# The last attention head taken out of the loop on two engines, with its last two modulation parts moved into the output tiles

## The chip, the cores and the metric

The kernel runs on one core of one Trainium2 chip. The metric is the device time of one execution in microseconds (us), shown as the median of several runs. The core's engines are TensorE (PE, matmuls; its weight loads are shown as PEld), VectorE (DVE), ScalarE (ACT), GpSimd (POOL) and SyncE (SP, which here only issues transfers). Each works through its own list of instructions and waits for the others at semaphores.

## The reference

Two layers of a diffusion backbone over 256 latent and 256 context tokens of width 2048: a neighbourhood attention with 16 heads, then a Mamba-2 SSD mixer, then an RMS norm. Each layer first derives shift, scale and gate from a conditioning vector:

```
mod = silu(c) @ ada_w + ada_b;  shift, scale, gate = split(mod, 3)
h = rms_norm(x, norm_w) * (1 + scale) + shift
x = x + gate * mixer(h)          # attention: (o * silu(z)) @ w_out
```

All is float32. `ada_w` of a layer is 2048 x 6144. The modulation of the second layer (and the gate of the first) does not depend on x.

## The kernel before, in words

Every large product is made of three matmuls with operands split into a rounded high part and the rest. A weight tile of 2048 x 128 is loaded by SP into a raw slot (1 MB), ACT copies it rounded into `w_hi` (`split_hi`, L353 and L901), DVE subtracts to get `w_lo` (`split_lo`, L357), and PE runs 48 matmuls per tile (`project`, L373, L375, L377), k = 0 to 15 with three each. Tiles 0 to 63 are q, k, v and z of the 16 heads, tiles 64 to 79 the output projection. Two raw slots, two `w_hi` and two `w_lo` are used in turn; tile 66 goes through a pair of its own, `w_third` (L945 on ACT, L1544 on DVE).

Beside these tiles a second piece of work runs that needs no PE. The modulation matrix-vector products are made in units of 512 columns, one unit per head, eight parts per unit. For part l, POOL issues the 512 KB load (`load_ada`, L605), DVE adds the latent half into `ada_acc` (`ada_part(l)`, L1415 and L1421, two instructions), ACT scales the context half into `ada_prod` (`products(l)`, L858, two instructions), and POOL adds those two rows into `acc` (`add_products(l)`, L614 or L620). There is one `ada_prod`, so `products(l)` waits until POOL has added part l - 1 (semaphore `s_gp`); `load_ada(l)` waits until both DVE and ACT have read part l - 2. The counters run through all units, so the order must be kept. After unit h, `ada_sums(h)` (L1432, L1436) reduces both accumulators.

Heads 1 to 15 (counted from 0) are issued one per turn: in turn i of the loop the projections of head i are made while the attention of head i - 1 is finished. Turns 2 to 15 are a hardware loop on each engine (`head` on ACT and DVE, `head_sums` on POOL). Behind the loop comes the seam to the output projection. There ACT copies the gated attention output rounded into `act_hi` (L953, one instruction for each k), DVE subtracts into `act_lo` (`o_low`, L1527), and the attention of head 15 (scores, softmax, exponentials, transposes, values) is done in between. PE runs tile 64 for k = 0 to 14 as `act_lo` comes, turns the probabilities (L2100, L2104), runs tile 65 for k = 0 to 14 with the values of head 15 (L2115) in its middle, and closes both with k = 15. Each output tile t then has an `out_tile` on DVE (`split_lo` of tile t + 1 from the third on, then the residual update L1562) and on ACT (`split_hi` of the next, copy of x L969, square L972). POOL adds the squares (L693) behind a memset of their sum (L688). One unit of modulation, unit 16, is spread over output tiles 0 to 7: `ada_part(t)` and `products(t)` behind tile t.

The order on each engine is written out by hand; there is no scheduler.

Of the kernel before, what the change touches and what calls it, by code (L numbers as in the profile page):

```python
# [27 lines left out]
KT = D // P  # L28
# [6 lines left out]
HEADS = 16  # L35
# [76 lines left out]
def trunk(nc, x, c, ctx, c_ctx, na_norm_w, na_ada_w, na_ada_b, na_w_in, na_rpb, na_w_out,  # L112
# [3 lines left out]
    with es:  # L116
# [275 lines left out]
        def backwards(v):  # L392

            return v.rearrange("p (r w) -> p r w", w=GRID_W)[:, :, ::-1]
# [370 lines left out]
        def _(act):  # L765
            step = Steps(act, act_step)
# [63 lines left out]
            def z_tanh_a(last):  # L830
                act.wait_ge(s_used, last.at(4))
                nc.scalar.activation(z_th, bank[1][:, :], ACT.Tanh, scale=0.5).then_inc(s_th, 1)
# [35 lines left out]
                act.wait_ge(s_vtr, i)  # L868
                nc.scalar.activation(v_hi.rearrange("p a b -> p (a b)"), bank[3][:, :], ACT.Copy).then_inc(s_vhi, 1)

            def head(t1, t4):

                i = t1.i
                z_tanh_a(Turn(i, 4, -4))
                split_hi(act, 1 + 4, Turn(i, 4, -4), 1, i * 32 + (16 - 16 * PRE // 2))
                exp_scores(Turn(i, 3, -3))
                products(0, t1)
                act.wait_ge(s_used, t4.at(1))
                nc.scalar.activation(q_hi, backwards(bank[0][:, :]), ACT.Copy, scale=QSCALE).then_inc(s_qhi, 1)
                next_hi(2, t4)  # L880
                turned_probs(Turn(t1.i, 1, -1))
                v_high(i)
                for l in range(1, 4):
                    products(l, t1)
                act.wait_ge(s_used, t4.at(2))
                nc.scalar.activation(k_hi, bank[1][:, :], ACT.Copy).then_inc(s_khi_k, 1)
                next_hi(3, t4)
                for l in range(4, 6):
                    products(l, t1)
                act.wait_ge(s_used, t4.at(3))  # L890
                nc.scalar.activation(v_t, bank[0][:, :], ACT.Copy).then_inc(s_free[0], 1)
                next_hi(4, t4)
                for l in range(6, 8):
                    products(l, t1)

            def next_hi(j, t4):
# [33 lines left out]
                    products(l, Turn())  # L930

            first_heads()
            with act.Fori(2, HEADS) as i:
                head(Turn(i, 1), Turn(i, 4))
            for k in range(KT):
                if k == 8:
                    z_tanh_a(Turn(base=60))
# [13 lines left out]
                    act.wait_ge(s_used, N_OUT_A)  # L951
                act.wait_ge(s_og, k + 1)
                nc.scalar.activation(act_hi3[:, k, :], o_t[:, k, :], ACT.Copy).then_inc(s_ohi, 1)  # L953


            def gained(u, t2, i):
# [296 lines left out]
        def _(dve):  # L1253
            step = Steps(dve, dve_step)
# [215 lines left out]
                dve.wait_ge(s_khi_k, last1.at(1))  # L1470
                nc.vector.tensor_tensor(k_lo, src[:, :], k_hi.bitcast(F32), ALU.subtract).then_inc(s_free[1], 1)

            def head(t1, t4):
                i = t1.i
                l1, l3 = Turn(i, 1, -1), Turn(i, 3, -3)
                z_gate_a(l1)
# [14 lines left out]
                for l in range(4, 6):  # L1491
                    ada_part(l, t1)
                split_lo(dve, 4, t4, 0)
                for l in range(6, 8):
                    ada_part(l, t1)

            def first_heads():
# [22 lines left out]
                    ada_part(l, none)  # L1520

            first_heads()
            with step.loop(2, HEADS, 14) as i:
                head(Turn(i, 1), Turn(i, 4))
            def o_low(k):
                dve.wait_ge(s_ohi, k + 1)
                nc.vector.tensor_tensor(act_lo3[:, k, :], o_t[:, k, :], act_hi3[:, k, :].bitcast(F32),  # L1527
                                        ALU.subtract).then_inc(s_olo, 1)
# [4 lines left out]
            for k in range(6):  # L1533
                o_low(k)
            softmax(Turn(base=15))
            for k in range(6, KT - 1):
                o_low(k)
# [4 lines left out]
            v_low(Turn(base=15))  # L1542
            dve.wait_ge(s_hi, N_OUT_A + 3)
            nc.vector.tensor_tensor(w_third[1], raw[0], w_third[0].bitcast(F32), ALU.subtract).then_inc(s_lo, 1)  # L1544
            dve.wait_ge(s_gsum, 1)
            for s in range(2):
                ada_columns(0, s, mod_a[:, 2, s, :], colk[:, V_NAB + 32:V_NAB + 48]).then_inc(s_gate, 1)
# [19 lines left out]
            turned = region(30, 512)  # L1567
            last = Turn(HEADS, 1)
            out_tile(0, Turn(), None)
            ada_sums(HEADS - 2, turned)  # L1570
            ada_part(0, last)
            for t in range(1, 8):
# [829 lines left out]
```

## Time and profile before

| | us |
|---|---|
| median of 3 runs | 2068.76 (2068.4 to 2070.06) |
| the profiled execution, its own time | 2066.29 |
| its span in the trace | 2064.4 |
| PE busy | 2011.2 (97% of the span) |
| DVE busy | 1454.2 (70%) |
| ACT busy | 968.8 (47%) |
| POOL busy | 699.0 (34%) |
| PE share of the chain that ended last | 80% |

The span is what the trace covers; 1.89 us of the execution lie around it. In the trace a row stands for one instruction or for several alike, with its start, its duration, and in brackets the idle time ahead of it and who ended that. PE rows overlap: within a tile one matmul of 512 columns starts 0.23 us after the one before. The seam lies at about 863 to 906 us of the span, the first output tiles with modulation parts at 906 to 987 us.

### The profile page before, as it was taken

To read this page: it belongs to the slowest core of one execution; us is meant where nothing else is said; L and a number is where in the kernel's file an instruction comes from. 1 tells how busy PE (TensorE), PEld (TensorE's weight loads), DVE (VectorE), ACT (ScalarE), POOL (GpSimd) and SP (SyncE) were. 2 spreads that over 40 slices of the span, in tenths; PEclk is the share of its full clock that TensorE was granted. 3 is DMA by queue.
4 is the path that set the end of the run, shared out by engine and by line. 5 is a ranking of instruction groups with operands and counts; after the bars stand their busy time and mean duration, and the time that the engine had idled before them with its cause. 6 is when DMAs were issued, how large, how long until landed. Compare 5 with 4: busy or idle time off the path is not lost.

```text
span 2064.4 us, 30995 instructions
## 1 busy us (share of the span) xinstructions
PE 2011.2 (97%) x10458; PEld 1673.0 (81%) x10458; DVE 1454.2 (70%) x2076; ACT 968.8 (47%) x1398; POOL 699.0 (34%) x568
## 2 busy tenths in 40 slices
PE   5999999999999999999999999999999999999998
PEld 3568888888888888878878888888888888888886
DVE  5248787777777777774358878787878787788544
ACT  3244455444544445544365454445444544456443
POOL 1036566555555656526100221212212122120011
PEclk8999999999999999999999999999999999999999
DMA  9996666666666666655353654555555546456654
GB/s 352 342 263 168 179 176 167 172 173 178 177 172 177 173 179 177 148 155 149 107 148 100 161 141 133 140 139 137 132 140 143 148 117 161 127 144 208 226 183 152
DMA packets 422706, 349.23 MB, mean 169 GB/s; under 512 B 13600, under 2 KB 366464, under 8 KB 422016
## 3 DMA queue, kind: packets, MB, share of 16 engines
q1 hardware_dynamic: 397552, 273.43, 45.8%
q0 software_dynamic: 19968, 70.26, 14.2%
q10 hardware_dynamic: 5136, 4.89, 0.7%
q8 instruction: 28, 0.46, 0.1%
q14 instruction: 22, 0.18, 0.0%
HBM read 344.21 MB, written 4.33 MB: 169 GB/s over the span
## 4 chain that ended last, share of the span: by engine, by line
PE 80%; DVE 7%; issue 4%; ACT 3%; DMA 3%; SPq 1%; POOL 1%; DVEq 0%; ACTq 0%; POOLq 0%
PE bank L373 20%; PE bank L377 20%; PE bank L375 20%; DMA arena<-in_na_ada_w_dram 3%; PE bank L2316 3%; PE bank L2318 2%; PE bank L2317 2%; PE bank L2115 1%; DVE w_lo L357 1%; PE bank L2249 1%; ACT w_hi L353 1%; DVE arena L1654 1%; PE bank L2230 1%; PE bank L2030 1%; PE bank L2244 1%
## 5 line engine op out<-in xcount | busy, mean ns | idle before, releaser
L373 PE MATMUL bank<-act_hi,w_hi 128*128 128x512 f32 (+1 forms) x2448 | 903.0, 369 | 9.0 <-DVE w_lo L357 4.7
L377 PE MATMUL bank<-act_hi,w_lo 128*128 128x512 f32 (+1 forms) x2448 | 888.3, 363 | 0.0
L375 PE MATMUL bank<-act_lo,w_hi 128*128 128x512 f32 (+1 forms) x2448 | 888.1, 363 | 0.0
L357 DVE TENSOR_TENSOR w_lo<-arena,w_hi 128x2048 fp32r<-128x2048 f32 x184 | 440.3, 2393 | 272.5 <-ACT w_hi L353 209.1
L373 PEld LDWEIGHTS bank<-act_hi,w_hi 128*128 128x128 f32 x2448 | 462.8, 189 | 80.8 <-DVE w_lo L357 6.4
L377 PEld LDWEIGHTS bank<-act_hi,w_lo 128*128 128x128 f32 x2448 | 462.3, 189 | 73.4
L375 PEld LDWEIGHTS bank<-act_lo,w_hi 128*128 128x128 f32 x2448 | 463.0, 189 | 68.9
L620 POOL TENSOR_TENSOR acc<-acc,arena 128x512 f32<-128x512 f32 x224 | 328.0, 1464 | 123.1 <-ACT arena L858 113.8
L353 ACT ACTIVATE w_hi<-arena 128x2048 fp32r<-128x2048 f32 x138 | 262.9, 1905 | 88.1 <-PE bank L2318 77.9
L858 ACT ACTIVATE arena<-arena,cond_c 128x512 f32<-128x512 f32 x256 | 171.3, 721 | 253.1 <-POOL acc L620 152.5
L1421 DVE SCALAR_TENSOR_TENSOR arena<-arena,cond_c 128x512 f32<-128x512 f32 x240 | 244.1, 1017 | 59.7 <-DMA arena<-in_ssd_ada_w_dram 38.1
L728 POOL TENSOR_TENSOR arena<-arena 128x1024 f32<-128x1024 f32 x32 | 77.1, 2410 | 433.0 <-ACT arena L1060 403.6
L1654 DVE SCALAR_TENSOR_TENSOR arena<-arena,convc 128x512 f32<-128x512 f32 (+1 forms) x192 | 145.7, 759 | 21.3 <-ACT arena L1044 7.1
L1060 ACT ACTIVATE arena<-arena 128x1024 f32<-128x1024 f32 x32 | 33.9, 1060 | 153.2 <-DVE arena L1706 153.2
L2316 PE MATMUL bank<-w_hi,act_hi 128*128 128x512 f32 x256 | 101.1, 395 | 1.9 <-DVE w_lo L357 1.9
L2318 PE MATMUL bank<-w_hi,act_lo 128*128 128x512 f32 x256 | 99.8, 390 | 0.0
L2317 PE MATMUL bank<-w_lo,act_hi 128*128 128x512 f32 x256 | 99.7, 389 | 0.0
L717 POOL TENSOR_SCALAR_AFFINE_SELECT arena<-arena 128x256 f32<-128x256 f32 (+1 forms) x32 | 22.0, 721 | 205.6 <-ACT arena L1178 205.6
L734 POOL TENSOR_TENSOR acc<-acc,arena 128x256 f32<-128x256 f32 x32 | 71.1, 2222 | 43.4 <-ACT arena L1086 43.4
L901 ACT ACTIVATE w_hi<-arena 128x2048 fp32r<-128x2048 f32 x43 | 82.1, 1909 | 0.0
L1049 ACT ACTIVATE arena<-arena 128x512 f32<-128x512 f32 (+1 forms) x48 | 28.6, 596 | 113.7 <-DVE arena L1654 113.7
L605 POOL DMA_DIRECT2D arena<-in_ssd_ada_w_dram x96 | 68.5, 714 | 32.7 <-DVE arena L1421 27.2
(253 smaller groups left out, 2168.6 us busy)
## 6 DMA issues: line engine op xcount, KB each, us to landing
arena<-in_ssd_w_in_dram SPq DMA_DIRECT2D x81, 1024.0 KB, 5.9
arena<-in_na_w_in_dram SPq DMA_DIRECT2D x58, 1024.0 KB, 7.2
arena<-in_ssd_ada_w_dram POOLq DMA_DIRECT2D x96, 512.0 KB, 4.0
arena<-in_na_ada_w_dram SPq DMA_DIRECT2D x64, 512.0 KB, 8.1
arena<-in_ssd_w_out_dram SPq DMA_DIRECT2D x32, 1024.0 KB, 5.0
arena<-in_na_ada_w_dram POOLq DMA_DIRECT2D x32, 512.0 KB, 4.1
arena<-in_na_w_out_dram SPq DMA_DIRECT2D x16, 1024.0 KB, 6.2
arena<-cs_scr SPq DMA_DIRECT2D x64, 256.0 KB, 5.9
```

The lines of the kernel that those rows point to most:

```text
L353: nc.scalar.activation(w_hi[:, n0 % 2, :], raw[slot], ACT.Copy).then_inc(s_hi, 1)
L357: nc.vector.tensor_tensor(w_lo[:, n0 % 2, :], raw[slot], w_hi[:, n0 % 2, :].bitcast(F32), ALU.subtract).then_inc(s_lo, 1)
L373: nc.tensor.matmul(out[:, 0:cols], hi[:, w], act_hi3[:, k, 0:cols], start=(k == 0), stop=False)
L375: nc.tensor.matmul(out[:, 0:cols], hi[:, w], act_lo3[:, k, 0:cols], start=False, stop=False)
L377: mm = nc.tensor.matmul(out[:, 0:cols], lo[:, w], act_hi3[:, k, 0:cols], start=False, stop=(k == KT - 1))
L620: nc.gpsimd.tensor_tensor(acc[:, :], acc[:, :], prod[:, h, :], ALU.add).then_inc(s_gp, 1)
L858: m = nc.scalar.activation(prod[:, h, :], ada_buf[l % 2][:, h, :], ACT.Copy, scale=cond_c[:, k, 1:2])
L1421: m = nc.vector.scalar_tensor_tensor(ada_acc, ada_buf[l % 2][:, h, :], cond_c[:, k, 0:1], ada_acc, ALU.mult, ALU.add)
L1654: m = nc.vector.scalar_tensor_tensor(u, xp[:, 0:segs, k:k + LAT], col(48 + 48 * k), u, ALU.mult, ALU.add)
L2316: nc.tensor.matmul(b[:, :], hi, w_hi[:, n % 2, w], start=(k == 0), stop=False)
L2317: nc.tensor.matmul(b[:, :], hi, w_lo[:, n % 2, w], start=False, stop=False)
L2318: mm = nc.tensor.matmul(b[:, :], lo, w_hi[:, n % 2, w], start=False, stop=(k == IT - 1))
```

## The change

On ACT and DVE the loop ends one turn earlier, and the last turn (head 15) stands behind it as plain code with `parts=6`, so without parts 6 and 7 of its modulation unit. On ACT both parts now follow the copy of `act_hi` for k = 14, ahead of `split_hi` of tile 65. On DVE part 6 follows the `w_lo` of tile 66, and part 7 follows `out_tile(0)`, ahead of `ada_sums(14)`. PE, POOL and SP keep their instructions and their order.

```diff
@@ ACT @@
-            def head(t1, t4):
+            def head(t1, t4, parts=8):
...
-                for l in range(6, 8):
+                for l in range(6, parts):
                     products(l, t1)
...
-            with act.Fori(2, HEADS) as i:
+            with act.Fori(2, HEADS - 1) as i:
                 head(Turn(i, 1), Turn(i, 4))
+            head(Turn(HEADS - 1, 1), Turn(HEADS - 1, 4), 6)
             for k in range(KT):
...
                 nc.scalar.activation(act_hi3[:, k, :], o_t[:, k, :], ACT.Copy).then_inc(s_ohi, 1)
+                if k == KT - 2:
+                    for l in range(6, 8):
+                        products(l, Turn(HEADS - 1, 1))
@@ DVE @@
-                for l in range(6, 8):
+                for l in range(6, parts):
                     ada_part(l, t1)
...
-            with step.loop(2, HEADS, 14) as i:
+            with step.loop(2, HEADS - 1, 14) as i:
                 head(Turn(i, 1), Turn(i, 4))
+            head(Turn(HEADS - 1, 1), Turn(HEADS - 1, 4), 6)
...
             nc.vector.tensor_tensor(w_third[1], raw[0], w_third[0].bitcast(F32), ALU.subtract).then_inc(s_lo, 1)
+            ada_part(6, Turn(HEADS - 1, 1))
             dve.wait_ge(s_gsum, 1)
...
             out_tile(0, Turn(), None)
+            ada_part(7, Turn(HEADS - 1, 1))
             ada_sums(HEADS - 2, turned)
```

ACT in the seam, before, from the last copies of `act_hi` to the turned probabilities (L838 and L844 are the exponentials of head 15, L353 is `split_hi` of tile 65, L945 the `w_hi` of tile 66):

```order
L953 ACTIVATE act_hi<-arena 128x512 x4
L838 ACTIVATE arena,small<-bank,small 128x512 x2
L844 ACTIVATE arena,small<-bank,small 128x256 x2
L953 ACTIVATE act_hi<-arena 128x512 x3
L353 ACTIVATE w_hi<-arena 128x2048
L945 ACTIVATE rounded<-arena 128x2048
L865 ACTIVATE rounded<-bank 128x512 x3
```

The same place on ACT in the changed kernel (L858 are `products(6)` and `products(7)`; other lines have moved by one):

```order
L954 ACTIVATE act_hi<-arena 128x512 x4
L838 ACTIVATE arena,small<-bank,small 128x512 x2
L844 ACTIVATE arena,small<-bank,small 128x256 x2
L954 ACTIVATE act_hi<-arena 128x512 x3
L858 ACTIVATE arena<-arena,cond_c 128x512 x4
L353 ACTIVATE w_hi<-arena 128x2048
L946 ACTIVATE rounded<-arena 128x2048
L865 ACTIVATE rounded<-bank 128x512 x3
```

The four scalings of parts 6 and 7 stand directly ahead of the `split_hi` of tile 65.

DVE from `out_tile(0)` to the `split_lo` of tile 67, before (L1562 is the residual update of a tile, L1432 and L1436 `ada_sums(14)`, L1415 and L1421 modulation parts, L357 `split_lo`):

```order
L1562 SCALAR_TENSOR_TENSOR arena<-bank,mod_a,arena 128x256 x2
L1432 STREAM_TRANSPOSE arena<-arena 128x512
L1436 TENSOR_REDUCE bank<-arena 128x16
L1432 STREAM_TRANSPOSE arena<-acc 128x512
L1436 TENSOR_REDUCE bank<-arena 128x16
L1415 TENSOR_SCALAR arena<-arena,cond_c 128x512
L1421 SCALAR_TENSOR_TENSOR arena<-arena,cond_c 128x512
L1562 SCALAR_TENSOR_TENSOR arena<-bank,mod_a,arena 128x256 x2
L1421 SCALAR_TENSOR_TENSOR arena<-arena,cond_c 128x512 x2
L357 TENSOR_TENSOR w_lo<-arena,w_hi 128x2048
```

The same place on DVE in the changed kernel (L1568 is the residual update, L1425 and L1419 modulation parts, L1436 and L1440 `ada_sums(14)`):

```order
L1568 SCALAR_TENSOR_TENSOR arena<-bank,mod_a,arena 128x256 x2
L1425 SCALAR_TENSOR_TENSOR arena<-arena,cond_c 128x512 x2
L1436 STREAM_TRANSPOSE arena<-arena 128x512
L1440 TENSOR_REDUCE bank<-arena 128x16
L1436 STREAM_TRANSPOSE arena<-acc 128x512
L1440 TENSOR_REDUCE bank<-arena 128x16
L1419 TENSOR_SCALAR arena<-arena,cond_c 128x512
L1425 SCALAR_TENSOR_TENSOR arena<-arena,cond_c 128x512
L1568 SCALAR_TENSOR_TENSOR arena<-bank,mod_a,arena 128x256 x2
L1425 SCALAR_TENSOR_TENSOR arena<-arena,cond_c 128x512 x2
L357 TENSOR_TENSOR w_lo<-arena,w_hi 128x2048
```

Two instructions, part 7, have come in behind the first residual update; the rest keeps its order.

## Rows read from the trace of the kernel before

**Rows 1.** Waits of PE from 862 to 906 us: total, times, longest.
```profile
PE bank L373 <- DVE act_lo L1527: 1.5, 1, 1.5
PE bank L373 <- DVE w_lo L357: 1.3, 1, 1.3
```

**Rows 2.** Timeline of PE in the seam: start, duration, engine, line.
```profile
875.13 0.88 PE L2091 MATMUL bank<-rounded 128*128 128x256 f32 x6
...
881.61 0.50 PE L373 MATMUL bank<-act_hi,w_hi 128*128 128x512 f32 x1 [1.46 <-DVE act_lo L1527]
...
890.75 0.50 PE L373 MATMUL bank<-act_hi,w_hi 128*128 128x512 f32 x1 [1.27 <-DVE w_lo L357]
```

**Rows 3.** Timeline of DVE in the seam.
```profile
878.28 0.75 DVE L1367 TENSOR_TENSOR bank<-bank,arena 128x256 f32<-128x256 f32 x2
...
880.87 5.50 DVE L1527 TENSOR_TENSOR act_lo<-arena,act_hi 128x512 fp32r<-128x512 f32 x9
...
888.41 2.29 DVE L357 TENSOR_TENSOR w_lo<-arena,w_hi 128x2048 fp32r<-128x2048 f32 x1
```

**Rows 4.** Timeline of ACT in the seam.
```profile
866.02 1.34 ACT L858 ACTIVATE arena<-arena,cond_c 128x512 f32<-128x512 f32 x2 [1.00 <-DMA arena<-in_ssd_ada_w_dram]
870.98 1.34 ACT L858 ACTIVATE arena<-arena,cond_c 128x512 f32<-128x512 f32 x2 [3.61 <-POOL acc L620]
872.22 4.26 ACT L953 ACTIVATE act_hi<-arena 128x512 fp32r<-128x512 f32 x8
...
879.80 0.69 ACT L838 ACTIVATE arena<-bank,small 128x512 f32<-128x512 f32 x1 [0.27 <-DVE small L1372]
...
883.60 1.92 ACT L353 ACTIVATE w_hi<-arena 128x2048 fp32r<-128x2048 f32 x1
```

**Rows 5.** POOL: L620 over the whole run (ns), then one timeline row.
```profile
L620 POOL TENSOR_TENSOR acc<-acc,arena x224: 1284/1303/3242, 148.2 to 979.7; 128x512 f32<-128x512 f32 x112
867.53 3.41 POOL L620 TENSOR_TENSOR acc<-acc,arena 128x512 f32<-128x512 f32 x2 [0.90 <-ACT arena L858]
```

**Rows 6.** Timeline of DVE from the first output tile on.
```profile
896.79 0.26 DVE L1445 TENSOR_TENSOR mod_a<-bank,colk 128x16 f32<-128x16 f32 x2 [1.50 <-PE bank L2158]
...
905.04 0.88 DVE L1562 SCALAR_TENSOR_TENSOR arena<-bank,mod_a,arena 128x256 f32<-128x256 f32 x2 [3.83 <-PE bank L377]
...
909.16 1.66 DVE L1421 SCALAR_TENSOR_TENSOR arena<-arena,cond_c 128x512 f32<-128x512 f32 x1
...
911.54 1.52 DVE L1421 SCALAR_TENSOR_TENSOR arena<-arena,cond_c 128x512 f32<-128x512 f32 x2
915.35 2.29 DVE L357 TENSOR_TENSOR w_lo<-arena,w_hi 128x2048 fp32r<-128x2048 f32 x1 [2.29 <-ACT w_hi L353]
...
922.49 3.38 DVE L357 TENSOR_TENSOR w_lo<-arena,w_hi 128x2048 fp32r<-128x2048 f32 x1
```

**Rows 7.** Timeline of ACT, then of PE, at output tile 67.
```profile
912.18 1.32 ACT L858 ACTIVATE arena<-arena,cond_c 128x512 f32<-128x512 f32 x2
913.41 1.90 ACT L353 ACTIVATE w_hi<-arena 128x2048 fp32r<-128x2048 f32 x1
...
917.69 0.50 PE L373 MATMUL bank<-act_hi,w_hi 128*128 128x512 f32 x1
```

**Rows 8.** Loads: a POOL issue, an SP issue, L605's landings at 865-871 and 918-919.5 us.
```profile
911.45 0.71 POOL L605 DMA_DIRECT2D arena<-in_ssd_ada_w_dram  x1 [1.17 <-DVE arena L1421]
...
907.02 0.37 SPq L460 DMA_DIRECT2D arena<-in_na_w_out_dram  x1
...
DMA to landing us min/median/max: 4.0/4.0/4.1
...
DMA to landing us min/median/max: 6.8/6.8/6.8
```

**Rows 9.** Stretches: us, each engine's busy time, PEclk (granted clock), DMA share, GB/s.
```profile
28.00:32.00 4.00, 0.36 (x4) 0.00 (x0) 4.00 (x3) 1.48 (x1) 0.00 (x0) 0.93 1.08 367
...
48.00:52.00 4.00, 3.00 (x7) 2.42 (x8) 3.59 (x7) 4.00 (x8) 2.66 (x3) 0.51 1.06 388
```

More of the change, by code:

```diff
@@ L1471, in key_low, with head @@
                 nc.vector.tensor_tensor(k_lo, src[:, :], k_hi.bitcast(F32), ALU.subtract).then_inc(s_free[1], 1)
-            def head(t1, t4):
+            def head(t1, t4, parts=8):
                 i = t1.i
```

## The prediction

> **What bounds the kernel now.** I read the page's shares first: PE is busy for 97% of the span, so only what makes PE wait can be won or lost. The waits of PE in the seam come next [rows 1]. Two are long enough to matter: 1.5 us for an `act_lo` and 1.3 us for a `w_lo`. The timeline of PE places them [rows 2]: 881.61 is k = 6 of tile 64, 890.75 the first matmul of tile 65. The timelines of DVE and ACT give the reasons [rows 3, 4]. At 881.61 DVE was late: it began the softmax of head 15 (L1367) at 878.28, though the scores were there when L2091 ended at 876.01 (875.13 + 0.88), since it first had six `o_low` to do, and those had begun only behind part 7. At 890.75 DVE was late again: it began the `w_lo` of tile 65 at 888.41, and ACT had its `w_hi` ready at 885.52. So DVE sets the end of the seam, with ACT 2.9 us ahead of it. From 906 us on no PE wait is listed, but one place is tight: tile 67's first matmul starts at 917.69, and its `w_lo` ended at 917.64 (915.35 + 2.29) [rows 6, 7].
>
> **Part by part, the start of the seam.** Taking parts 6 and 7 off the last turn frees ACT and DVE some 5 us earlier. The first eight `act_hi` (L953), at 872.22 before, can run while PE is still in tile 63 and six `o_low` with them. The rest of `act_hi` waits for z as before. DVE is then free when the scores end, and the softmax starts at 876.06, 2.22 us earlier. The first wait of PE goes: `o_low` for k = 6, begun at 880.87, begins at 878.65 and ends at 879.33, and PE wants it at about 880.0 (881.61 less the wait of 1.46, and less a little for which the overlap of matmuls does not show). Gain there 1.5 to 1.7 us, if nothing else follows.
>
> **What is late next.** ACT follows the softmax: exponentials at 877.58 instead of 879.80, and it is done with k = 14 at 881.38, 2.22 us ahead of the 883.60 at which `split_hi` of tile 65 began [rows 4]. There now stand `products(6)` and `products(7)`, and between them ACT must wait for POOL to add part 6, since `ada_prod` is single. The old place shows the price whole: 866.02 to 870.98 from the one to the other, and 1.24 us more until ACT went on at 872.22, 6.20 us together, of which POOL's two adds are 3.41 [rows 4, 5]. So `split_hi` of tile 65 starts at 883.60 - 2.22 + 6.20 = 887.58. From a `split_hi` to the end of the `w_lo` behind it, with DVE waiting, takes 917.64 - 913.41 = 4.23 us [rows 6, 7]. That gives 891.81, and PE starts tile 65 at about 891.86 instead of 890.75: **1.11 us later**, with both old waits turned into one of some 4 us (PE is through with tile 64 and its transposes at 890.75 - 1.27 = 889.48 now, 1.6 earlier then). The bounds come from L620: two adds at its least, 1.284 us each, make the block 5.36 us and the shift +0.27; one at its largest, 3.242, with an ordinary one, makes it +2.3 [rows 5]. I take 3.41, what an add took at the old place, with DVE as busy beside it as it will be at the new one.
>
> Part 6 on DVE behind the `w_lo` of tile 66 costs 1.5 us (two L1421, 1.52) [rows 6]. It fits: DVE stood idle there for 1.50 us before L1445 and for two more before it gates the output, and the last `o_low` was ready 2.8 us before PE reached k = 15. Nothing, unless DVE is 3 us later than I think. POOL's list is unchanged, but its load for part 0 of unit 16 now waits for that part 6, and its add of part 7 comes behind it at about 900 us. ACT wants `ada_prod` again at 907 or later, so this costs nothing.
>
> **The output tiles.** Everything behind tile 64 is 1.11 us later. Then part 7 stands between `out_tile(0)` and `ada_sums(14)`: DVE ends it at 905.92 + 1.11 + 1.45 = 908.48. In the queue behind it are `ada_sums(14)`, part 0, `out_tile(1)`; ACT's square of tile 1, `products(1)` and `split_hi` of tile 67 wait for that one, and PE for the `w_lo`. With 0.05 us of slack, all 1.45 us reach PE: 1.11 + 1.45 = 2.56 us.
>
> A second thing waits for part 7: POOL's `load_ada(1)` of unit 16, since the slot is the one part 7 is read from. Before it was issued at 875 us and had 35 us to land. Now it is issued about 0.6 us behind part 7 (as 911.45 follows the end of part 0 at 910.82, 909.16 + 1.66), at 909.1. SP's 1 MB load of a weight tile, 907.02 before, goes out at 908.1, just ahead of it. How long the part's load takes is in the rows: 4.0 us with the transfers idle, 6.8 us for the one issued at 918.7, 0.8 us behind such a 1 MB load [rows 8]. I take 6.8, the nearer case: it lands at 915.9, where `products(1)` could have started at 912.18 + 2.56 = 914.7. So ACT starts it 3.7 us later than before, and the `w_lo` of tile 67 and PE with it: **+3.7 us** in all, the new PE wait there being 2.7 us. With 4.0 us it is +2.6, with 7.1 +4.0.
>
> The Trainium skill (Trainium Kernel Development and Optimization, Key Constraints) says that transfers from the SP and POOL queues run on the same engines and interleave. By that rule the load shares with the weight tile and the sum is the +3.7; by the idle landing alone it would be +2.6.
>
> Tile 68 recovers: its `w_lo` ended at 925.87, 3.1 us before PE wanted it (917.69 and 48 matmuls 0.23 us apart, 11.3 with the transposes of x), and the two chains move together [rows 6]. Beyond it PE never waits until the next seam, whose work hangs on PE's last output tile. So the shift stays to the end. PE, POOL and SP run the same instructions; the plain copy of the last turn saves and adds only register instructions, which I put at nothing.
>
> **Sum.** +1.1 (tile 65) +1.45 (part 7) +1.15 (landing) = +3.7 us. The profiled execution is 2066.29 us (1.89 around its span) and would be 2070.0; the median of the runs is 2.47 above that execution, so the forecast is 2068.76 + 3.7 = **2072.5 us**. By the bounds of its terms alone, 0.27 + 1.45 = +1.7 to 2.3 + 2.9 = +5.2.
>
> **Rivals.**
> A, the slower clock. PE's new wait, from about 888 to 891.9, comes behind the transposes of the probabilities (1.5 us), so over 5 us pass without a product. In the trace the granted clock fell from 2.4 to 1.2 GHz within the stretch 28 to 32 us (0.93 as its mean), where PE was busy for 0.36 of 4 us, and it was still at half for nearly all of the 3.00 us of PE work at 48 to 52 us [rows 9]. Against it, PE waits less here than there, and the transposes are work too. If the clock falls, 2 to 5 us of work at half rate add 1 to 2.5 us, I take 1.8: +5.5, 2074.3 us. The Trainium skill (TensorE: Matmul & The Clock Gate, Part 4: PE-mode transpose and Why this matters for your kernels) says transposes don't count as busy for the gate and warns of gaps between bursts; by that it would fall here, and the sum would be the +5.5.
> B, the quick landing: the load of part 1 takes about 4 us, the weight tile not being in its way. +2.6, 2071.4 us.
> C, the faster side. ACT had 2.9 us in hand at tile 65. If its block of two parts fitted into them, DVE would carry its 2.22 us through to PE and PE would start tile 65 at 888.5: -2.2; with the load landing early enough and the square of tile 1 not on the path, part 7 would cost nothing, and the time would be 2066.5 us. The start of tile 65 turns from earlier to later at a block of 2.9 + 2.2 = 5.1 us. For it: DVE, and not ACT, sets the end of the seam now. Against it: two scalings of 1.34 and the adds between make 5.36 at the very least.
> D, nothing moves: one of my two chains is read wrongly and gains and losses cancel, 2068.8 us.
>
> **Chances.** Forecast 0.40, A 0.32, B 0.15, C 0.05, D 0.08. A measurement tells about 0.2%, 4.1 us, from no change. The forecast lies just below that (0.3 of it above), A almost wholly above, B and D within. Slower by over 0.2%: 0.12 + 0.30 + 0.03 = 0.45. Faster: C alone stays within, so only with something I have missed, 0.04. Within: 0.51. The range, from B less the spread of the medians (2068.4 to 2070.06) to A at its dearer end: 2070.0 to 2076.3.
>
> **What would show it.** In the profile of the changed kernel: no wait for `act_lo` near 880; softmax of head 15 at 876; four L858 between `act_hi` and `split_hi` of tile 65, with an idle time of about 3.5 us on ACT inside; one PE wait of 3 to 4 us for `w_lo` ahead of tile 65, starting at about 891.9; a PE wait of 1.4 to 3 us ahead of tile 67 at about 921.4, with ACT's `products(1)` released by the load; the clock of the stretch 891 to 895, 1.00 for the forecast, 0.5 for A. Wrong would be a PE that starts tile 65 before 890.7, or a wait at tile 68 or later.

## The result: 0.48% slower, 9.7 us

The changed kernel takes 2079.22 us (median of 6 runs, 2074.76 to 2082.12), the kernel before 2069.55 (6 runs, 2068.4 to 2070.86): ratio 1.0048, 95% interval 1.0038 to 1.0058. The forecast was 2072.5 us, and its range ended at 2076.3. The sign was right, the size was not: less than half of the loss was in the sum. The profiled execution of the kernel before lies 3.3 us below its median, that of the changed kernel 0.3 us above its own.

| | before | after |
|---|---|---|
| median, us | 2069.55 | 2079.22 |
| profiled execution, us | 2066.29 | 2079.52 |
| its span, us | 2064.4 | 2077.9 |
| granted clock, mean | 0.991 | 0.988 |
| PE waits from 862 to 935 us | 2.8 us [rows 1] | 8.6 us |

These are the waits of PE in the changed kernel, in the same view (total, times, longest). Two of PE's three waits are longer than any before, and the third (ahead of the transposes of the probabilities) stands where there was none:

```profile
PE bank L373 <- DVE w_lo L357: 7.3, 2, 4.0
PE bank L2107 <- DVE arena L1389: 1.3, 1, 1.3
```

The timeline of PE says where they are; the rows answer to [rows 2] and to the last of [rows 7]:

```profile
877.87 0.88 PE L2098 MATMUL bank<-rounded 128*128 128x256 f32 x6
...
890.34 1.09 PE L2107 MATMUL bank<-ident,arena 128*128 128x128 f32 x8 [1.32 <-DVE arena L1389]
...
895.08 0.79 PE L373 MATMUL bank<-act_hi,w_hi 128*128 128x512 f32 x1 [3.21 <-DVE w_lo L357]
...
927.65 0.80 PE L373 MATMUL bank<-act_hi,w_hi 128*128 128x512 f32 x1 [4.04 <-DVE w_lo L357]
```

Since PE runs the same list in both kernels, the difference between the starts of one and the same instruction in the two traces is a ledger of the change. Each line is one such instruction; the last column is what the stretch in front of it added.

| PE instruction | before | after | later by | added |
|---|---|---|---|---|
| last scores of head 15 | 875.13 | 877.87 | 2.74 | 2.74 |
| first matmul of tile 65 | 890.75 | 895.08 | 4.33 | 1.59 |
| sums for the modulation | 896.42 | 902.32 | 5.90 | 1.57 |
| first matmul of tile 67 | 917.69 | 927.65 | 9.96 | 4.06 |
| the next sums | 997.49 | 1009.70 | 12.21 | 2.25 |
| head of the SSD stage | 1266.65 | 1277.41 | 10.76 | -1.45 |
| end of its loop | 1715.89 | 1729.54 | 13.65 | 2.89 |

**The first line is not the change's.** 1.4 us of it arose behind a wait of 2.7 us at 141 us, which both kernels have, and after which the clock fell in one of the two executions. The stretch 138 to 144 us of the kernel before, and the same of the changed one (columns as in [rows 9]):

```profile
138.00:144.00 6.00, 3.31 (x15) 2.48 (x14) 5.97 (x6) 5.05 (x6) 3.12 (x4) 1.00 0.99 196
```
```profile
138.00:144.00 6.00, 3.29 (x10) 2.32 (x9) 5.97 (x6) 4.82 (x6) 4.00 (x4) 0.73 0.89 172
```

Of the 13 profiles of this study, all with the same code there, the clock fell at that place in 9 and stayed at 2.4 GHz in 4, and the profile of the kernel before is one of the 4. From there to the seam before_pad (below), which has none of the moves, took 1.4 us longer than the profile of the kernel before, and the changed kernel 1.6. The -1.45 us is no gain of the change either: before_pad has -1.46 over the same stretch. That leaves 12.4 us in this trace for the change, against 9.7 by the medians.

**Tile 65.** ACT's block stands where the forecast put it. Timelines of ACT, POOL and DVE, the rows that answer to [rows 3 to 5]:

```profile
884.12 1.34 ACT L858 ACTIVATE arena<-arena,cond_c 128x512 f32<-128x512 f32 x2
889.56 1.33 ACT L858 ACTIVATE arena<-arena,cond_c 128x512 f32<-128x512 f32 x2 [4.10 <-POOL acc L620]
890.80 1.89 ACT L353 ACTIVATE w_hi<-arena 128x2048 fp32r<-128x2048 f32 x1
```
```profile
885.62 3.85 POOL L620 TENSOR_TENSOR acc<-acc,arena 128x512 f32<-128x512 f32 x2 [16.41 <-ACT arena L858]
```
```profile
887.02 2.74 DVE L1386 TENSOR_SCALAR arena<-arena,small 128x512 f32<-128x512 f32 x2
...
892.73 2.29 DVE L357 TENSOR_TENSOR w_lo<-arena,w_hi 128x2048 fp32r<-128x2048 f32 x1 [1.85 <-ACT w_hi L353]
```

From 884.12 to 890.80 the block takes 6.68 us (forecast 6.20); POOL's two adds are 3.85 (forecast 3.41). These 0.44 us more are nearly all by which tile 65 missed the forecast (1.59 for 1.11). The adds run beside DVE's normalising of the probabilities, which takes 2.74 us for two instructions; over the whole run the same line has (ns, least, middle, most):

```profile
L1386 DVE TENSOR_SCALAR arena<-arena,small x32: 469/486/1502, 161.1 to 888.3; 128x512 f32<-128x512 f32 x32
```

The rows of tile 65's `w_lo` say that DVE then waited 1.85 us for ACT's `w_hi`, so it is ACT's block, and not the normalising, that sets tile 65. The probabilities come late by the normalising, and most of the 2.2 us won at the softmax is gone by PE's transposes, for which PE waits 1.32 us: they start 2.38 us after those of the kernel before, 0.36 less than the 2.74 at the seam's head.

**Tile 67.** ACT, then DVE, the rows that answer to [rows 6, 7], then POOL's load of part 1 of unit 16 with its time to landing, and what stands behind that load in POOL's list:

```profile
915.24 0.63 ACT L976 ACTIVATE arena<-arena 128x512 f32<-128x512 f32 x1 [4.47 <-POOL arena L688]
...
920.05 0.63 ACT L976 ACTIVATE arena<-arena 128x512 f32<-128x512 f32 x1 [2.47 <-DVE arena L1568]
920.73 1.34 ACT L858 ACTIVATE arena<-arena,cond_c 128x512 f32<-128x512 f32 x2
921.97 1.90 ACT L353 ACTIVATE w_hi<-arena 128x2048 fp32r<-128x2048 f32 x1
```
```profile
911.74 1.53 DVE L1425 SCALAR_TENSOR_TENSOR arena<-arena,cond_c 128x512 f32<-128x512 f32 x2
...
916.13 1.41 DVE L1419 TENSOR_SCALAR arena<-arena,cond_c 128x512 f32<-128x512 f32 x1
...
920.73 3.60 DVE L1425 SCALAR_TENSOR_TENSOR arena<-arena,cond_c 128x512 f32<-128x512 f32 x2 [0.71 <-DMA arena<-in_ssd_ada_w_dram]
924.25 3.34 DVE L357 TENSOR_TENSOR w_lo<-arena,w_hi 128x2048 fp32r<-128x2048 f32 x1
```
```profile
913.90 0.71 POOL L605 DMA_DIRECT2D arena<-in_ssd_ada_w_dram  x1 [8.72 <-DVE arena L1425]
914.61 0.54 POOL L688 MEMSET arena<- 128x512 f32 x1
915.96 1.29 POOL L693 TENSOR_TENSOR arena<-arena 128x512 f32<-128x512 f32 x1 [0.81 <-ACT arena L976]
```
```profile
DMA to landing us min/median/max: 6.8/6.8/6.8
```

The load is issued behind part 7 and lands 6.8 us later, at 920.7, as forecast. Counted from the modulation sums, ACT's `split_hi` of tile 67 starts 2.66 us later than before, and the forecast had 2.6 for this place. That it fits is luck, for the load is hardly in it: ACT came to the square of tile 1 only at 920.05 and began `products(1)` 0.68 us behind that, against 0.54 before. What made the rest was on DVE: part 7 took 1.56 us, and the first instruction of part 0 took 1.41 us where it had taken 0.48. It ran beside POOL's addition of tile 0's squares. That addition came so late because POOL's list has the memset (L688) behind `load_ada(1)`, and so behind part 7, and ACT's first square waited 4.47 us for it.

Two more things are new behind that: DVE's part 1 waits 0.71 us for the load and takes 3.60 us where it took 1.52, so the `w_lo` starts 0.4 us behind the end of its `w_hi` (923.87), and it takes 3.34 us in place of 2.29. Together 1.4 us more than the 2.6.

**The clock.** Behind both waits PE works at half rate (1.2 in place of 2.4 GHz) for 3 to 5 us. Stretches of the changed kernel; in the kernel before, PEclk is 1.00 in every stretch from 888 to 936 us:

```profile
894.00:896.00 2.00, 0.92 (x2) 0.83 (x3) 2.00 (x3) 1.95 (x4) 0.00 (x0) 0.76 0.00 0
896.00:898.00 2.00, 2.00 (x6) 1.52 (x5) 2.00 (x4) 0.00 (x0) 0.00 (x0) 0.50 0.54 142
898.00:900.00 2.00, 2.00 (x10) 1.60 (x9) 2.00 (x2) 0.00 (x0) 0.00 (x0) 0.88 1.14 327
...
928.00:930.00 2.00, 2.00 (x6) 1.52 (x6) 1.79 (x3) 1.59 (x3) 0.87 (x1) 0.50 0.54 185
930.00:932.00 2.00, 2.00 (x6) 1.60 (x5) 0.00 (x0) 2.00 (x2) 2.00 (x2) 0.50 0.94 270
932.00:934.00 2.00, 2.00 (x9) 1.57 (x8) 1.90 (x1) 0.07 (x1) 1.92 (x2) 0.85 1.09 287
```

Six matmuls in 2 us at 0.50, nine or ten at 0.85 and 0.88. What the clock withheld from tile 65 on is 2 us times the missing share of each stretch, 0.48 + 1.0 + 0.24 = 1.7 us, and the ledger has 1.57; behind tile 67 (0.35 us of a stretch at 0.50, then these three) it is 0.2 + 1.0 + 1.0 + 0.3 = 2.5, and the ledger has 2.25.

**The SSD stage.** This is DVE's loop of six turns from 1204 us on, and none of its instructions changed. Yet from its second turn on it lost 0.5 to 0.6 us in each, five times, the first of them 390 us behind the last moved instruction. DVE's waits in the changed kernel, the first instruction of the loop in one turn, and the page's row on instruction transfers:

```profile
DVE arena L1687 <- issue: 2.8, 5, 0.6
```
```profile
1302.72 0.42 DVE L1687 COPY arena<-bank 128x256 f32<-128x256 f32 x1 [0.59 <-issue]
```
```profile
q14 instruction: 48, 0.39, 0.1%
```

"issue" is idle time in which the engine waited for nothing that the profile shows. The kernel before has no such wait at that line, and its q14 row reads 22 packets and 0.18 MB. By my count the last turn written out puts 51 more instructions into DVE's stream ahead of the SSD loop.

### The profile page after: what moved, and what is told of

It reads as the page before. It is cut to its first block, busy times and chain, and to the rows that moved or that the text cites. A ratio compares the mean times of both kernels' runs of the same rounds, so it can differ in the third digit from the quotient of the medians.

```text
span 2077.9 us, 30951 instructions
## 1 busy us (share of the span) xinstructions
PE 2017.8 (97%) x10458; PEld 1678.2 (81%) x10458; DVE 1454.6 (70%) x2076; ACT 968.8 (47%) x1398; POOL 702.5 (34%) x568
## 3 DMA queue, kind: packets, MB, share of 16 engines
HBM read 344.21 MB, written 4.33 MB: 168 GB/s over the span
## 4 chain that ended last, share of the span: by engine, by line
PE 73%; DVE 11%; issue 6%; ACT 5%; DMA 3%; DVEq 1%; SPq 1%; POOL 0%; ACTq 0%; POOLq 0%
PE bank L373 18%; PE bank L377 18%; PE bank L375 18%; DVE arena L1661 3%; PE bank L2323 3%; DMA arena<-in_na_ada_w_dram 3%; PE bank L2325 2%; PE bank L2324 2%; DVE w_lo L357 2%; ACT w_hi L353 2%; PE bank L2122 2%; PE bank L2256 1%; PE bank L2037 1%; PE bank L2094 1%; PE bank L2010 1%
## 5 line engine op out<-in xcount | busy, mean ns | idle before, releaser
L357 DVE TENSOR_TENSOR w_lo<-arena,w_hi 128x2048 fp32r<-128x2048 f32 x184 | 439.9, 2391 | 274.5 <-ACT w_hi L353 210.8
L620 POOL TENSOR_TENSOR acc<-acc,arena 128x512 f32<-128x512 f32 x224 | 329.8, 1472 | 137.6 <-ACT arena L858 128.2
L353 ACT ACTIVATE w_hi<-arena 128x2048 fp32r<-128x2048 f32 x138 | 263.0, 1906 | 87.3 <-PE bank L2325 77.8
L858 ACT ACTIVATE arena<-arena,cond_c 128x512 f32<-128x512 f32 x256 | 171.4, 721 | 251.6 <-POOL acc L620 154.6
L1425 DVE SCALAR_TENSOR_TENSOR arena<-arena,cond_c 128x512 f32<-128x512 f32 x240 | 243.0, 1012 | 61.0 <-DMA arena<-in_ssd_ada_w_dram 39.7
L605 POOL DMA_DIRECT2D arena<-in_ssd_ada_w_dram x96 | 68.5, 714 | 53.7 <-DVE arena L1425 48.3
```

Source lines behind the costliest of these rows:

```text
L353: nc.scalar.activation(w_hi[:, n0 % 2, :], raw[slot], ACT.Copy).then_inc(s_hi, 1)
L357: nc.vector.tensor_tensor(w_lo[:, n0 % 2, :], raw[slot], w_hi[:, n0 % 2, :].bitcast(F32), ALU.subtract).then_inc(s_lo, 1)
L620: nc.gpsimd.tensor_tensor(acc[:, :], acc[:, :], prod[:, h, :], ALU.add).then_inc(s_gp, 1)
L858: m = nc.scalar.activation(prod[:, h, :], ada_buf[l % 2][:, h, :], ACT.Copy, scale=cond_c[:, k, 1:2])
L1425: m = nc.vector.scalar_tensor_tensor(ada_acc, ada_buf[l % 2][:, h, :], cond_c[:, k, 0:1], ada_acc, ALU.mult, ALU.add)
```

## Experiments

Each was timed in 5 rounds against the kernel before on the same chip. "Pads" are instructions that only raise a semaphore that nothing waits for, on DVE ahead of the last two output tiles; they move the code behind them.

**unroll_only**, the last turn written out, all parts at their old place:

```diff
-            with step.loop(2, HEADS, 14) as i:
+            with step.loop(2, HEADS - 1, 14) as i:
                 head(Turn(i, 1), Turn(i, 4))
+            head(Turn(HEADS - 1, 1), Turn(HEADS - 1, 4))
```

> The last turn stands outside the loop on ACT and DVE as in the change, but parts 6 and 7 stay in it at their old place, ahead of the seam. Theory 1 (code position): the plain turn puts 51 more instructions ahead of DVE's SSD loop, the loop of 310 instructions then falls across one code block more, and its first block has to be fetched again at each turn: DVE idle for 'issue' of 0.5 to 0.6 us at the first line of the loop in five turns, about 48 instruction packets on q14 instead of 22, and +2.5 to +3 us, so 2072 to 2073. The seam and the output tiles look as before. Rival (the moved parts are all): no issue rows, 22 packets, no change within 1 us.

2071.49 us (2069.07 to 2073.57), ratio 1.0004 (0.9995 to 1.0013). By the time it can't be told from no change; in the trace the effect is plain: 48 packets, idle time at the loop's first line five times, and 3.27 us lost from 1266 to 1716 us. At the seam nothing moves.

**before_pad**, the kernel before with 51 pads and nothing else:

```diff
+            for _ in range(51):
+                dve.sem_inc(s_pace, 1)
             end = Turn(base=KT - 2)
```

> The kernel before with 51 increments of an unused semaphore put into DVE's list near the end of the output tiles, where it idles 6.5 us; nothing else. Theory 1: the SSD loop starts at the same instruction number (670) as in the change, so the same five issue rows and the same +2.5 to +3 us. Rival (it is the plain turn itself, or chance): no change within 1 us, no issue rows.

2073.3 us (2070.67 to 2077.73), ratio 1.0015 (1.0006 to 1.0024). The page's row and DVE's wait in it:

```profile
q14 instruction: 48, 0.39, 0.1%
```
```profile
DVE arena L1682 <- issue: 3.0, 5, 0.7
```

Two of PE's rows at tile 64 in this trace, and a stretch behind them:

```profile
880.08 0.47 PE L373 MATMUL bank<-act_hi,w_hi 128*128 128x512 f32 x1 [1.47 <-DVE act_lo L1527]
...
881.68 0.80 PE L373 MATMUL bank<-act_hi,w_hi 128*128 128x512 f32 x1 [0.67 <-DVE act_lo L1527]
```
```profile
882.00:884.00 2.00, 2.00 (x6) 1.52 (x6) 2.00 (x5) 2.00 (x5) 0.26 (x1) 0.50 0.60 147
```

Place alone does it: 3.13 us lost in the loop with no instruction of the change. This trace shows something else besides: its seam, unchanged code, took 3.07 us longer than that of the profile before. The softmax started at 883.96, 3.1 us later than in [rows 3] after the 2.6 us that this execution was late already, because `products(6)` (871.73) had waited for a load that landed late. PE's waits at tile 64 were 1.1 us longer in all for it, three in place of one. The rest is the clock: behind the waits of 1.47 and 0.67 us, with three matmuls between them, it was at 0.86, 0.50 and 0.79 in three stretches of 2 us, 1.7 us withheld. So the seam of the kernel before has a price that varies from one execution to the next, and its clock can fall too. Of the two profiles with all parts at their old place, unroll_only has the seam of the profile before to 0.01 us and this one is dearer.

**after_pad**, the changed kernel with 60 pads, which put the SSD loop elsewhere again:

```diff
+            for _ in range(60):
+                dve.sem_inc(s_pace, 1)
             end = Turn(base=KT - 2)
```

> The changed kernel with 60 such increments more at that place, so that the SSD loop starts at 730 and its start and end fall into two code blocks again. Theory 1: the five issue rows are gone, q14 back near 22 to 24 packets, and 2.5 to 3 us less than the changed kernel, about 2076.5. Rival: the time of the changed kernel, 2079.

2075.93 us (2074.42 to 2079.01), ratio 1.0034 (1.0022 to 1.0046): 2.9 us less than the 1.0048 of the changed kernel. 23 packets, no idle time at the loop's head. The seam repeats: +3.23 us from the last scores to the sums (the changed kernel: 3.16). From there to 997 us it is +4.31 against 6.31. Up to there the two kernels are the same code; this time DVE's part 1 took 2.46 us and the `w_lo` of tile 67 2.49. act_back (+6.29) and dve_alone (+4.41), which have ACT's parts at their old place and are the same code as each other up to there, show the same two prices.

**act_back**, the changed kernel with ACT's two products at their old place, so that only DVE's parts are moved:

```diff
-            head(Turn(HEADS - 1, 1), Turn(HEADS - 1, 4), 6)
+            head(Turn(HEADS - 1, 1), Turn(HEADS - 1, 4))
...
-                if k == KT - 2:
-                    for l in range(6, 8):
-                        products(l, Turn(HEADS - 1, 1))
```

> The changed kernel with products(6) and products(7) on ACT at their old place in the last turn; DVE's parts stay moved. Theory 1 (ACT's two parts with the add between them hold split_hi of tile 65): PE's waits ahead of the probability transposes and of tile 65 shrink to under 1.5 us, tile 65 starts 2 us earlier against the start of the seam than in the kernel before, and no clock fall there; the wait at tile 67 for part 7 and the late load stays, 2 to 4 us; SSD loop with its issue rows. About 2074. Rival (DVE's own parts and its contention with POOL set the seam): tile 65 still starts late, 2078 or more.

2075.46 us (2071.43 to 2079.82), ratio 1.0028 (1.002 to 1.0037), the loop's 48 packets included. In its trace tile 65 starts 2.1 us earlier than before, counted from the last scores, with no wait left at tile 64, and tile 67 costs 6.3 us. So the loss at tile 65 is ACT's and that at tile 67 DVE's.

**act_alone**, only ACT's products moved, 60 pads:

```diff
-            ada_part(6, Turn(HEADS - 1, 1))
...
-            ada_part(7, Turn(HEADS - 1, 1))
```

(from the changed kernel; its DVE head call has all 8 parts again, and the pads are those of after_pad)

> Only ScalarE's parts are moved as in the change; VectorE's stay ahead of the seam; the last turn is written out and 60 semaphore-only instructions keep the SSD loop at 22 packets. Theory (ScalarE's block, waiting for GpSimd's add, holds split_hi(65), PE stands still over 3 us at tile 65, and the clock falls behind it): one PE wait of 3.2 us or more for w_lo at tile 65, granted clock under 0.8 in the 2 us behind it, +3.6 us between tile 64 and the modulation sums; total +3.6 us, ratio 1.0017. Rival (the forecast's price, the block costs what it waits and the clock stays): +1.1 us, ratio 1.0005, clock 1.00.

2071.23 us (2068.49 to 2077.33), ratio 1.0016 (1.0007 to 1.0024). PE's waits from 862 to 935 us, and a stretch behind the first:

```profile
PE bank L373 <- DVE w_lo L357: 3.7, 1, 3.7
PE bank L2107 <- DVE arena L1389: 1.5, 1, 1.5
```
```profile
896.00:898.00 2.00, 2.00 (x6) 1.57 (x5) 2.00 (x4) 0.00 (x0) 0.00 (x0) 0.50 0.59 149
```

+3.95 us from the last scores to the sums, nothing from there to 997 us: the theory's 3.6, not the forecast's 1.1. The time says 3.3 us.

**dve_alone**, act_back with 60 pads:

> Only VectorE's parts are moved as in the change; ScalarE's stay ahead of the seam; last turn written out, 60 semaphore-only instructions as in the other kernels. Theory (part 7 between out_tile(0) and the sums pushes the chain part 7, load, memset, square, block product, w_hi, w_lo of tile 67 late; PE waits 4 us and the clock falls; against it tile 64 starts 1.85 us earlier): PE waits 2.5 to 4 us at tile 67, clock near 0.5 for 4 us behind it, +4.3 to +6.3 us there, -1.85 at tile 64; total +2.5 to +4.5 us, ratio 1.0012 to 1.0021. Rival (the forecast's prices 1.45 and 1.15 for tile 67 and no clock fall, with the gain at tile 64): +0.7 us, ratio 1.0003, clock 1.00.

2069.7 us (2066.62 to 2072.38), ratio 1.0005 (0.9996 to 1.0013). Again a wait and a fall at tile 67, PE's waits and a stretch:

```profile
PE bank L373 <- DVE w_lo L357: 4.1, 2, 2.8
PE bank L373 <- DVE act_lo L1529: 1.6, 1, 1.6
```
```profile
924.00:926.00 2.00, 2.00 (x7) 1.59 (x6) 2.00 (x1) 2.00 (x2) 2.00 (x2) 0.54 1.01 287
```

+4.4 us at that place in the trace, and this time no gain at tile 65 (+0.1 us): a load ahead of the seam had landed 2.2 us later against PE than in act_back (`products(6)` at 869.77, there 867.49), and the products still ahead of `act_hi` pass that on. The time fits the rival's +0.7 better than the theory's +2.5 to +4.5; the trace fits the theory at tile 67, not at tile 64. act_back less the loop's 0.0015 is 1.0013, this is 1.0005: what DVE's move costs over many executions is 1 to 3 us and stays that open.

**part7_early**, the changed kernel with 60 pads and part 7 directly behind part 6:

```diff
             ada_part(6, Turn(HEADS - 1, 1))
+            ada_part(7, Turn(HEADS - 1, 1))
...
             out_tile(0, Turn(), None)
-            ada_part(7, Turn(HEADS - 1, 1))
             ada_sums(HEADS - 2, turned)
```

> The changed kernel with VectorE's part 7 directly behind part 6, where the profile of the changed kernel shows VectorE idle for 1.6 us ahead of the sums, in place of behind out_tile(0); 60 semaphore-only instructions keep the SSD loop at 22 packets. Theory (the place of part 7 makes the loss at tile 67): unit 16's second load is issued about 9 us earlier, the load and part 1 of unit 16 are in time, PE's wait at tile 67 is gone or under 0.5 us, clock 1.00 there; what is left is tile 65's 3.6 us less the 1.85 us at tile 64; total +1.8 to +3 us, ratio 1.0008 to 1.0015. Rival (tile 67 is late by the contention of ScalarE, VectorE and GpSimd in the output tiles or by tile 65's delay itself): a wait of over 2 us stays at tile 67, ratio 1.003 or more, as with part 7 in its changed place.

2070.12 us (2068.39 to 2074.16), ratio 1.001 (1.0001 to 1.0019). The load of part 1 is issued at 903.2 and lands in 4.0 us, the wait at tile 67 is gone, and tile 65 starts as late as it did (+1.57). The clock stayed low for longer behind it: 2.82 us up to the sums, where the changed kernel lost 1.57. PE's waits from 862 to 935 us and a stretch:

```profile
PE bank L373 <- DVE w_lo L357: 3.2, 1, 3.2
PE bank L2109 <- DVE arena L1389: 1.4, 1, 1.4
```
```profile
896.00:898.00 2.00, 2.00 (x6) 1.59 (x5) 2.00 (x2) 0.00 (x0) 0.00 (x0) 0.50 1.13 324
```

One line moved takes 0.0024 off after_pad's ratio, 5 us (two chips; in the traces it is +4.31 us there against -0.02). So it is the place of part 7 that loses tile 67. The stretching of DVE by POOL there hangs on that place: here the memset comes ahead of the output tiles, at 903.9, and the first instruction of part 0 takes 0.48 us again.

**slots_pad**, all four parts in idle stretches ahead of the softmax, 60 pads:

```diff
@@ ACT, behind act_hi(k) @@
+                if k == 3 or k == 7:
+                    products(6 + k // 4, Turn(HEADS - 1, 1))
@@ DVE, behind o_low(k) @@
+                if k == 3 or k == 5:
+                    ada_part(6 + k // 5, Turn(HEADS - 1, 1))
```

> The last head's parts 6 and 7 of unit 15 go into gaps that the profiles show: ScalarE's block products (6) behind act_hi(3) and (7) behind act_hi(7), VectorE's part 6 behind o_low(3) and part 7 behind o_low(5), both ahead of the softmax; 60 semaphore-only instructions on VectorE move the SSD loop so that it takes the 22 instruction packets of the kernel before. Theory (the cost is where the parts were put, the gain is the wait for act_lo at tile 64, 1.5 us, and what hangs on it, 1.85 us in the profile with ScalarE's part back): no wait at tile 64, the two waits of tile 65 as before (about 1.5 and 1.1), none at tile 67, clock 1.00 from 870 to 940; 2.0 us faster than before, ratio 0.9990 (0.998 to 1.000). Rival (whatever leaves the place ahead of the seam comes back as delay of the softmax or of unit 16's loads): a wait of over 1 us at tile 65 or 67 more than before, and 0 to +3 us, ratio 1.000 to 1.0015.

2067.8 us (2066.28 to 2069.12), ratio 0.9997 (0.9988 to 1.0006): no loss, and no gain either, against the theory's 2 us. DVE in its timeline:

```profile
877.05 3.83 DVE L1424 SCALAR_TENSOR_TENSOR arena<-arena,cond_c 128x512 f32<-128x512 f32 x2
880.80 0.75 DVE L1370 TENSOR_TENSOR bank<-bank,arena 128x256 f32<-128x256 f32 x2
```

Part 7 took 3.83 us beside POOL's additions, not 1.5, and the softmax started 2.4 us behind the scores (2.3 before). PE's two waits are those of before, 1.6 and 1.3 us. The rival's mechanism was right, a delay of the softmax; the longer waits at tile 65 or 67 that it named did not come. The gap was filled with something that grows.

**gap_a_pad, gap_b_pad and gap_b** keep ACT's `products(6)` ahead of the seam and put `products(7)` behind `act_hi(7)`. DVE's part 7 goes to its place in part7_early; part 6 stays ahead of the seam in gap_a_pad and goes with part 7 in gap_b_pad and gap_b. gap_b has no pads. The edit of gap_b from the changed kernel:

```diff
@@ ACT @@
-            head(Turn(HEADS - 1, 1), Turn(HEADS - 1, 4), 6)
+            head(Turn(HEADS - 1, 1), Turn(HEADS - 1, 4), 7)
...
-                if k == KT - 2:
-                    for l in range(6, 8):
-                        products(l, Turn(HEADS - 1, 1))
+                if k == 7:
+                    products(7, Turn(HEADS - 1, 1))
@@ DVE @@
             ada_part(6, Turn(HEADS - 1, 1))
+            ada_part(7, Turn(HEADS - 1, 1))
...
             out_tile(0, Turn(), None)
-            ada_part(7, Turn(HEADS - 1, 1))
```

> ScalarE's products(6) stay ahead of the seam as in the kernel before, products(7) come behind act_hi(7); VectorE's part 6 stays ahead of the seam, part 7 comes behind w_lo of the third tile (where part7_early had it); 60 semaphore-only instructions keep the SSD loop at 22 packets. Theory (what ties up VectorE between the seam's head and the softmax is the cost, 2.2 us of it recoverable; GpSimd's additions then lie beside act_lo and not beside the normalising): softmax starts with the scores, no wait for act_lo at tile 64, the normalise of two rows takes 0.9 us and not 2.7, tile 65 about 1.9 us earlier than in the kernel before counted from the seam, no wait over 0.5 us at tile 67, clock 1.00 from 870 to 940; 2 us faster than before, ratio 0.999. Rival (as in slots_pad, the saving is eaten in place by longer VectorE instructions beside GpSimd's additions or by a late load): tile 65 where it was before, 0 to +1 us, ratio 1.0000 to 1.0005.

> As gap_a_pad, but VectorE's part 6 too comes behind w_lo of the third tile, with part 7. Theory: VectorE is free ahead of the seam as in act_back, where tile 65 came 1.85 us earlier; the first load of unit 16 goes out some 30 us later than before, and is still in time for its use behind the sums; -2 us, ratio 0.999; no wait over 0.5 us at tile 67, clock 1.00. Rival (two parts, 3.1 to 4.8 us on VectorE, behind the third tile delay the modulation columns and the gating of the last head): a PE wait at the sums or at the last attention tile, 0 to +2 us, ratio 1.000 to 1.001.

> gap_b_pad without the 60 semaphore-only instructions, so VectorE's SSD loop starts 51 instructions later than in the kernel before and 60 earlier than in gap_b_pad. Theory (the loop's place in the instruction stream costs 0.5 to 0.7 us in each of its five turns): instruction packets 48 in place of 23, idle time with nothing waited for of 0.5 to 0.6 us at the loop's first instruction in each turn, +3 us against gap_b_pad, ratio to it 1.0015, against before 1.0005. Rival (the 60 instructions themselves or chance made the difference between the padded and unpadded kernels): same time as gap_b_pad within 0.7 us.

gap_a_pad: 2066.73 us (2064.0 to 2069.16), ratio 0.9988 (0.9979 to 0.9997). gap_b_pad: 2065.65 (2062.67 to 2070.16), 0.9987 (0.9978 to 0.9996). gap_b: 2068.76 (2066.76 to 2071.48), 0.9998 (0.9989 to 1.0007). The two padded ones beat both kernels: that before by 0.12 and 0.13%, with intervals that end just below 1, the changed one by 0.6%. DVE in gap_b_pad, then PE's only wait from 862 to 935 us, then the stretch behind it:

```profile
879.49 0.77 DVE L1370 TENSOR_TENSOR bank<-bank,arena 128x256 f32<-128x256 f32 x2 [2.54 <-PE bank L2099]
...
887.71 0.88 DVE L1385 TENSOR_SCALAR arena<-arena,small 128x512 f32<-128x512 f32 x2
```
```profile
PE bank L373 <- DVE w_lo L357: 0.9, 1, 0.9
```
```profile
890.00:900.00 10.00, 9.05 (x54) 7.29 (x53) 9.83 (x10) 1.75 (x4) 1.37 (x2) 1.00 0.40 107
```

The softmax waits for the scores (2.54 us, released by PE), the normalising takes its 0.88 us, and tile 65 comes 2.2 us earlier than before, counted from the seam's head. gap_b differs from gap_b_pad by the pads alone, and gives 3.1 us back, which its trace has in the loop:

```profile
DVE arena L1686 <- issue: 3.2, 5, 0.8
```

## Why the prediction was wrong

**Right**: the softmax earlier by 2.2 us and the first PE wait gone; four L858 ahead of `split_hi` of tile 65, with 4.1 us of idle time inside (forecast 3.5); the long PE waits at tiles 65 and 67, for the `w_lo` each (at tile 65 it came in two pieces, 1.32 us ahead of the transposes and 3.21 behind them); the load of part 1 issued behind part 7, landing after 6.8 us and not 4.0 (rival B falls); no further wait up to 935 us.

**The failed step, 2.9 us in the trace**: "the plain copy of the last turn saves and adds only register instructions, which I put at nothing". The copy is 51 instructions of DVE's stream by my count, and they moved the SSD loop to a place at which each of its five jumps back is followed by idle time. before_pad shows it with nothing else changed; in after_pad and gap_b_pad pads take it away. The time of after_pad, 2075.93 us, lies inside the range of the forecast. By times alone it is 0.0004, 0.0015, 0.0014 and 0.0011 in the four comparisons, 2.3 us on average, and only before_pad has an interval that leaves out no change; by the traces it is 2.9 to 3.4 us in all five kernels with 48 packets, and none in the eight with 22 to 24. The rows say that packets double and that the idle time sits at the loop's first instruction; that the idle time is the wait for those packets is read from the two together. The Trainium skill (Runtime: NRT & Kernel Launch, Instruction fetch mechanics) says that a taken branch whose target is outside the window held by the engine forces a fetch before execution goes on; the traces agree, with 0.5 to 0.9 us at a jump back. I did not weigh this rule, though the change touched a loop.

**The clock, 3.8 us**: I gave rival A 1.8 us, and 0.32, for tile 65 alone; measured 1.57. That was the likelier case, not the rival: in the four profiled executions with that block the clock fell four times, for 1.6, 1.6, 1.6 and 2.8 us. The second fall, at tile 67 (2.25 us), stood in no case, although the forecast itself had a new wait of 2.7 us there. The transposes of the probabilities were rightly in the argument, and still the chance was set below one half.

**Mis-sized terms, 1.9 us**: tile 65 +1.59 for +1.11, by POOL's adds at 3.85 for 3.41; tile 67 +4.06 for the +2.6 of part 7 and landing, by DVE's part 1 at 3.60 for 1.52 and a `w_lo` at 3.34 for 2.29. In each of these rows DVE and POOL work at the same time, and the same instructions are short where the other is idle. I had priced POOL's adds beside DVE, and never DVE beside POOL.

**A path that I had wrong, and luck in the 2.6**: the landing's 1.15 us hardly reached ACT (at most 0.14 us, 0.68 - 0.54); DVE's wait of 0.71 us for it is in the last 1.4. In its place DVE's part 0 took 0.93 us more, through a path that the prediction does not have: part 7, POOL's load, the memset behind it, ACT's first square, POOL's addition beside part 0. The square waits 4.45 to 4.47 us for that memset in all four kernels with part 7 behind `out_tile(0)`, and not in part7_early.

**Sum of the trace**: 1.59 + 1.57 + 4.06 + 2.25 + 2.89 = 12.4 us. The medians differ by 9.7. Two things can make up the difference: a seam that was cheap in the profile of the kernel before (3.07 us dearer in before_pad, the same in unroll_only), and a tile 67 that was dear in that of the changed one (2.0 us cheaper in after_pad and 1.9 in dve_alone). How often each is dear was not measured, so the shares stay open.

Rivals C and D fall. C's condition (the block in 5.1 us or less) did not hold: 6.68.

## What to carry to other kernels

Price a move by the waits that it makes PE take close together: here single waits of 1.3 to 1.6 us cost themselves, but one of 1.47 us with one of 0.67 close behind it was followed by a fallen clock (before_pad), and those of 2.7 us and more at tiles 65 and 67 were in eight cases out of eight, in the changed kernel 1.6 and 2.3 us on top. Look at the stream behind the change: writing out a turn moves every later loop, and 60 idle instructions won back 3 us in the traces. Follow what waits for the moved part on every engine: POOL's load waited, and so did the memset behind it. Read two profiles of the kernel before, if there are two: one shows its waits and clock as they fell that time. A part set in a gap of one engine should be checked against what the sharing engine does at that moment: the same two instructions took 1.5 us in one gap and 3.8 in the other.

## What the hardware showed that I had not expected

- DVE loops of the same instructions, at another place in the stream: 22 to 24 packets or 48, and with 48 0.5 to 0.9 us idle at each jump back.
- A PE wait of 2.7 us, same code, same place: the clock fell to 1.2 GHz in 9 executions of 13 and stayed in 4, worth 1.4 to 1.6 us.
- Two pairs of kernels with the same code up to 997 us: in each pair tile 67 cost 6.3 us in one execution and 4.3 or 4.4 in the other.
- Two TENSOR_SCALAR of 128x512 took 2.74 us beside POOL's additions and 0.88 alone (gap_b_pad), POOL's two additions 3.85, where one takes 1.284 at its least [rows 5].
